# A decoder step with a streamed mixture of experts: six expert slots instead of five, the residual rows parked in memory, the conditioning weights in half blocks

## What is computed

```python
mod = silu(c) @ w_ada + b_ada                   # 1024 x 6144: shift, scale, gate, twice
h = rmsnorm(x, g1) * (1 + sc1) + sh1
z = h @ w_in                                    # 1024 x 2048: conv gates B and C, value v, S5 input u
y_conv = B * conv3(C * v)
y_ssm = glu(gelu(s5(u)))                        # 32 groups, 64 complex states, scan over positions
x = x + gt1 * (concat(rmsnorm(y_conv), rmsnorm(y_ssm)) @ w_out)
h = rmsnorm(x, g2) * (1 + sc2) + sh2
x = x + gt2 * moe(h)                            # top 1 of 4 groups, then top 2 of 8 experts in it
y = rmsnorm(x, final_g)
```

## Time and profile before

| | |
|---|---|
| time, three runs | 652.00, 662.49, 662.91 us; median 662.49 us |
| the profiled execution | 654.28 us, of which the span from first to last instruction is 652.5 us |
| TensorE: busy, mean granted clock | 519.0 us (80% of the span), 0.914 |
| DVE, ACT, POOL busy | 268.3, 111.7, 81.9 us |
| moved by DMA | 168.96 MB, mean 259 GB/s; 414 to 419 GB/s in the slices from 392 to 587 us but one (412) |
| chain that ended last | PE 49%, DMA 26%, SP's queue 11%, DVE 8% |

### The profile page before, as it was taken

The page is one execution under the profiler, slowest core; times in us unless marked ns, Lnnn a source line. Parts: engine busy times, 40 slices in busy tenths (PEclk is TensorE's granted clock), DMA queues, the critical chain, the costliest instruction groups (busy, mean ns, idle before and its releaser), DMA issues.

```text
span 652.5 us, 8666 instructions
## 1 busy us (share of the span) xinstructions
PE 519.0 (80%) x3412; PEld 311.5 (48%) x3412; DVE 268.3 (41%) x603; ACT 111.7 (17%) x205; POOL 81.9 (13%) x117
## 2 busy tenths in 40 slices
PE   0658999988999979999933999977787878768291
PEld 0546898867788856445532344333232323223040
DVE  6429928894163351574555222222121202111246
ACT  4502171110000343222212001010000001000012
POOL 4020003000011320210012021111111111100001
PEclk9977999999999979999955899999797979979786
DMA  8995037757598878010196499999999999994343
GB/s 293 331 303 224 1 131 74 256 200 303 177 248 30 224 288 341 0 41 32 38 383 258 161 396 414 414 416 417 417 416 416 419 412 416 415 416 201 119 181 137
DMA packets 33545, 168.96 MB, mean 259 GB/s; under 512 B 6572, under 2 KB 8828, under 8 KB 22160
## 3 DMA queue, kind: packets, MB, share of 16 engines
q1 hardware_dynamic: 26128, 150.69, 62.7%
q0 software_dynamic: 7376, 17.71, 8.9%
HBM read 161.89 MB, written 13.18 MB: 268 GB/s over the span
## 4 chain that ended last, share of the span: by engine, by line
PE 49%; DMA 26%; SPq 11%; DVE 8%; issue 2%; POOL 1%; ACT 1%; DVEq 0%; POOLq 0%; ACTq 0%
DMA arena<-in_w_ada 11%; PE bank L1400 11%; DMA arena<-in_w_exp 10%; PE bank L1646 10%; PE bank L1537 7%; SPq L425 6%; SPq L417 5%; PE bank L1675 4%; PE bank L1384 3%; DMA arena<-in_w_in 3%; PE bank L1528 2%; PE bank L1702 2%; DVE arena L859 1%; PE bank L1629 1%; PE bank L1578 1%
## 5 line engine op out<-in xcount | busy, mean ns | idle before, releaser
L1646 PE MATMUL bank<-arena 128*64 128x512 f32 x512 | 126.2, 649 | 31.7 <-DMA arena<-in_w_exp 30.6
L1400 PE MATMUL bank<-arena 128*128 128x272 f32 x512 | 122.3, 400 | 3.9 <-DMA arena<-in_w_in 3.9
L1400 PEld LDWEIGHTS bank<-arena 128*128 128x128 f32 x512 | 98.0, 193 | 25.9 <-DMA arena<-in_w_in 4.2
L859 DVE TENSOR_TENSOR arena<-arena 128x16 f32<-128x16 f32 (+12 forms) x196 | 93.7, 478 | 23.6 <-ACT arena L728 13.7
L1646 PEld LDWEIGHTS bank<-arena 128*64 128x64 f32 x512 | 43.3, 149 | 113.3 <-issue 99.7
L1675 PE MATMUL bank<-arena 128*64 128x512 f32 x256 | 58.5, 597 | 11.8 <-DVE arena L1283 11.8
L1275 DVE TENSOR_TENSOR arena<-arena,bank 128x256 f32<-128x256 f32 x16 | 6.7, 422 | 142.6 <-ACT arena L814 142.6
L1537 PE MATMUL bank<-arena 128*128 128x512 f32 x128 | 56.7, 596 | 0.0
L1384 PE MATMUL bank<-arena 128*32 128x128 f32 x768 | 28.2, 310 | 34.0 <-DMA arena<-in_w_ada 31.5
L591 POOL DMA_INDIRECT expert_rows<-arena x16 | 16.1, 1009 | 219.9 <-DVE arena L1291 205.1
L1384 PEld LDWEIGHTS bank<-arena 128*32 128x32 f32 x768 | 24.8, 126 | 37.9 <-issue 23.2
(11 more groups left out here) (180 smaller groups left out, 446.7 us busy)
## 6 DMA issues: line engine op xcount, KB each, us to landing
arena<-in_w_exp SPq DMA_DIRECT2D x64, 1024.0 KB, 22.9
arena<-in_w_exp SPq DMA_DIRECT2D x64, 512.0 KB, 19.4
arena<-in_w_ada SPq DMA_DIRECT2D x12, 2048.0 KB, 9.0
arena<-in_w_in SPq DMA_DIRECT2D x4, 2048.0 KB, 12.0
arena<-in_w_out SPq DMA_DIRECT2D x2, 2048.0 KB, 16.6
arena<-expert_rows SPq DMA_DIRECT2D x4, 1024.0 KB, 8.2
arena<-in_x_prompt SPq DMA_DIRECT2D x4, 512.0 KB, 7.6
arena<-in_x_prompt POOLq DMA_DIRECT2D x4, 512.0 KB, 12.4
```

What stands on the lines that cost most here:

```text
L859: link(V.tensor_tensor(out, a, b, op))
L1400: ins = mm(bk[:, 0:HTOK], w[:, k, P * f:P * (f + 1)], hT[:, k, HTOK * h:HTOK * (h + 1)], start=(k == 0), stop=(k == KT - 1))
L1646: ins = mm(out[CAP * e:CAP * (e + 1), :], x[:, 4 * h + kk, CAP * e:CAP * (e + 1)], slot[(2 * c + e) % NSLOT][h][:, kk, :], start=(h == 0 a ...
```

## The change

1. **Front loads at once.** `ada(3)` gets a buffer of its own (at 133) and the first block of `w_in` another (at 80, the later place of the matrix `T`), so that SP issues the first five blocks without a wait, and the small late loads go behind the second block of `w_in`. POOL zeroes `T` only after `zu` has read the block there; before, it did so at the start.
2. **Halves through a ring.** `ada(4)` to `ada(11)` are loaded as two halves of 1 MB each into a ring of three places of 8 KB. SP waits less often for the block just before; PE waits for a half at a time.
3. **Constants first.** POOL builds the routing constants ahead of the root of the branch norms, and DVE prepares the token numbers ahead of its wait for that root.
4. **Six slots.** Behind each `h2` store POOL also stores the tile's rows `x1` in memory (`x1_rows`). Their place becomes most of a sixth slot, loaded ahead after SP has seen all five stores. At the end of the expert stage SP loads the rows back (`x1_back`, into slot 4) after the 15th pair's `down`, and ACT and DVE use these.
5. **ACT asks for down weights.** From the seventh expert on SP issues only gate and up loads; ACT issues a coming pair's four down loads after its copy `y_half` of the pair that frees the place.

```diff
-NSLOT = 5
+NSLOT = 6
...
-STREAM = [("ada", 0, 0, None), ("ada", 1, 1, None), ("ada", 2, 2, None), ("ada", 3, 0, ("ada", 0)), ("in", 0, 1, ("ada", 1)),
+STREAM = [("ada", 0, None, "b0", None), ("ada", 1, None, "b1", None), ("ada", 2, None, "h0", None), ("ada", 3, None, "late", None),
+          ("in", 0, None, "T", None), ("ada", 4, 0, "h0", ("ada", 2)), ("ada", 4, 1, "h1", ("ada", 2)),
...
-        block_buf = [at(16 * b, KT, 512) for b in range(NBUF)]
+        block_buf = {"b0": at(0, KT, 512), "b1": at(16, KT, 512), "h0": at(32, KT, 512), "h1": at(40, FT, 512),
+                     "h2": at(137, FT, 512), "T": at(80, KT, 512), "late": at(133, KT, 512)}
...
-                slot_at(116, 133, 124, 141)]
+                slot_at(116, 133, 124, 141), slot_at(149, 157, 165, 177)]
...
+        x1_back = [at(k, D) for k in (116, 120, 124, 133, 137)]
...
                 for k in range(NSLOT, NE):
                     sp.wait_ge(gu_done, count(p, (k - NSLOT) // 2 + 1))
                     load(k)
-                    sp.wait_ge(down_done, count(p, (k - NSLOT) // 2 + 1))
-                    load_down(k)
+                sp.wait_ge(down_done, count(p, PAIRS - 1))
+                sp.dma_start(at(116, 2, D), x1_d[0:2 * P, :].rearrange("(i p) d -> p i d", i=2)).then_inc(x1_landed, 16)
+                for i, (t0, n) in enumerate(TILES):
+                    if i >= 2:
+                        sp.dma_start(x1_back[i][0:n, :], x1_d[t0:t0 + n, :]).then_inc(x1_landed, 16)
...
             load(4)
             load_down(4)
+            sp.wait_ge(x1_stored, 16 * 5)
+            load(5)
+            load_down(5)
             load_rest(0)
...
-            pool.memset(T, 0.0).then_inc(T_zero, 1)
...
+            wait_full(pool, job("zu", (FT - 1, 1)))
+            pool.memset(T, 0.0).then_inc(T_zero, 1)
...
                 pool.dma_start(h2_d[t0:t0 + n, :], h2[p % 2][0:n, :]).then_inc(h2_stored[p % 2], 16)
+                pool.dma_start(x1_d[t0:t0 + n, :], x1[0:n, i, :]).then_inc(x1_stored, 16)
...
+            def load_next_down(c):
+
+                for k in (2 * c + NSLOT, 2 * c + 1 + NSLOT):
+                    if k < NE:
+                        s = k % NSLOT
+                        for h in range(2):
+                            a = KT * 512 + D * h
+                            act.dma_start(slot[s][2 + h], t["w_exp"][k][:, a:a + D]).then_inc(down_full[s], 16)
...
                     y_half(p, c)
+                    load_next_down(c)
...
+                    if c >= 4 and k % FT == 0:
+                        w = block_at("ada", c, k // FT)
```

More of the change, by code:

```diff
@@ L302, in build @@
         par_in, conv_in, wr_in, x_again = (sem(n) for n in ("par_in", "conv_in", "wr_in", "x_again"))
-        block_in = [sem(f"block_in{b}") for b in range(NBUF)]
+        block_in = {b: sem(f"block_in_{b}") for b in BUFS}
         late_row_in = sem("late_row_in")
@@ L398, in quarters @@
                     sp.dma_start(dst[32 * j:32 * (j + 1), :, :], src[0:1, :, j, :].partition_broadcast(32)).then_inc(done, 16)
-            for kind, c, b, after in STREAM:
+            for kind, c, part, b, after in STREAM:
                 if after is not None:
                     wait_full(sp, job(*after))
-                kts = FT if kind == "glu" else KT
+                kts = FT if kind == "glu" or part is not None else KT
                 src = t["w_glu"] if kind == "glu" else t["w_" + kind][c]
+                if part is not None:
+                    src = src[:, FT * 512 * part:FT * 512 * (part + 1)]
                 sp.dma_start(block_buf[b][:, 0:kts, :], src.rearrange("p (k n) -> p k n", k=kts)).then_inc(block_in[b], 16)
@@ L408, in _ @@
                     quarters(g1_q, t["g1"], 2, row_in)
-                if kind == "ada" and c == 2:
+                if kind == "in" and c == 1:
                     quarters(late_bias, t["b_ada"][:, 4 * 512:12 * 512], 8, late_row_in)
@@ L453, in _ @@
                     sp.wait_ge(pass_open, p + 1)
-                    for k in range(NSLOT):
+                    load(0)
+                    load_down(0)
+                    sp.wait_ge(x1_landed, p * 64)
+                    for k in range(1, NSLOT):
                         load(k)
@@ L544, in _ @@
             pool.dma_start(br, t["b_router"]).then_inc(wr_in, 16)
-            pool.wait_ge(msm_ready, 1)
-            pool.tensor_tensor(rstd_m, ms_m, half, ALU.pow).then_inc(mrstd_ready, 1)
+            wait_full(pool, job("ss", 0))
             link(pool.memset(tri, 1.0))
@@ L558, in _ @@
             pool.sem_inc(moe_consts, 1)
+            pool.wait_ge(msm_ready, 1)
+            pool.tensor_tensor(rstd_m, ms_m, half, ALU.pow).then_inc(mrstd_ready, 1)
             for p, i in enumerate(ORDER):
@@ L1346, in finish @@
                 dve.wait_ge(rstd2_ready, i + 1)
-                V.scalar_tensor_tensor(out=x2[i][0:rows, :], in0=x1[0:rows, i, :], scalar=rstd[0:rows, i:i + 1],
+                V.scalar_tensor_tensor(out=x2[i][0:rows, :], in0=x1_back[i][0:rows, :], scalar=rstd[0:rows, i:i + 1],
                                        in1=fg[0:rows, :], op0=ALU.mult, op1=ALU.mult).then_inc(y_ready, 1)
@@ L1372, in _, with block_at @@
             open_job.next = 0
-            def block_at(kind, c=0):
-                b, uses = BLOCK_OF[(kind, c)]
+            def block_at(kind, c=0, part=None):
+                b, uses = BLOCK_OF[(kind, c, part)]
                 pe.wait_ge(block_in[b], 16 * uses)
```

34 lines of the change are left out of this document (21 added, 13 removed).

## The result

The changed kernel takes 633.55 us (median of four runs, 633.4 to 640.3) against 660.35 for the kernel before in the same group of runs: a ratio of 0.967 (0.962 to 0.972). The ratios, with their 95% intervals, are estimated from the fast runs of both kernels and are not the quotient of the two medians. The forecast was 641.8, range 633 to 654.

A forecast was written before the change was run, and what follows sets the result against it. TensorE was taken to bind half of the end, late loads the rest, with DMA binding the expert stage. 654.28 - 7.5 - 5.7 - 0.6 - 7.6 + 6.0 - 1.4 + 4.3 = 641.8 us, range 633 to 654.

The forecast's parts named there:

- the forecast's own case: Whole kernel: all terms come as summed, 641.8 us, counted as 638 to 647; chance 0.43.
- the first rival: Expert stage: sixth slot pays in full, gather slips through, ends keep cover; 631.5 us; in full or part, chance 0.29.
- front loads at once: Front: fourth conditioning block and w_in land earlier, first projection at 43.65 instead of 51.20 us; -7.5 us.
- ring of halves: Projections: second halves always land within a part's 7.5 us, so eight cycles take 75.7 instead of 81.4 us; -5.7.
- sixth slot, bytes: Expert stage: one expert's 3.15 MB no longer pass while the stream bounds, at 416 GB/s; -7.6 us.
- first gather slower: Before the expert stage: first gather meets the sixth slot's loads, 10.1 us instead of 4.1; +6.0 us.
- start of the stream: Expert stage's start: SP no longer holds gate and up loads behind a wait for down; -1.4 us (0 to -2.7).
- order at the end: Expert stage's end: fewer bytes left to cover PE's last two pairs; +4.3 us, between 0 and 7.4.
- so down weights run ahead: Expert stage: ACT's queue isn't served behind SP's, leaving only 4.2 MB instead of 7.3 near the end.
- Front or ring keep less: Front and projections: w_in behind POOL's tiny loads, halves slow as blocks; 651.0, one alone 645.3 or 647.5; chance 0.20.
- No sixth load ahead: Expert stage: last x1 store lands after the first gate_up, so no bytes ahead, no slower gather; 643.4 us; chance 0.03.
- ACT stalls: Expert stage: four issues block ACT above 10.2 us, delaying silu and copies; at 3.5 us each, 691 us; chance 0.05.

The follow-up runs named there:

- e4: Changed kernel with the eight small late loads back behind the third conditioning block, ahead of the fourth: 641.41 us, ratio 0.969.
- e5: Changed kernel with both halves of a conditioning block waiting until the whole block ahead of them is done: 636.28 us, ratio 0.974.
- e2: Changed kernel with five slots, no sixth expert loaded ahead: 639.64 us, ratio 0.968.
- e3: Changed kernel with the sixth slot's loads held back until PE has turned the first gathered rows: 632.18 us, ratio 0.954.
- e10: Kernel before, with only ACT asking for the down weights added: 654.03 us against 658.38, ratio 0.993.
- e1: Changed kernel with SP asking for the down weights too, in the old order: 635.38 us, ratio 0.962.
- e9: Changed kernel unaltered, run once more in another group of runs: 636.65 us against 658.38 for the kernel before, ratio 0.967.
- e7: Changed kernel with the residual rows read back after the last gate_up, not the 15th down: 635.91 us, ratio 0.972.
- e6: Changed kernel with SP asking for all weights, both experts of a pair at once, ACT for none: 635.54 us, ratio 0.972.
- e8: Changed kernel with SP asking for all in pairs, sixth slot loaded after the first gather, rows read back after the last gate_up: 629.92 us, ratio 0.963.
- e11: Changed kernel with SP asking for all in pairs and sixth slot loaded after the first gather, rows read back as before: 629.76 us, ratio 0.957.
- e12: Changed kernel with SP asking in pairs, sixth slot after the first gather, rows read back late, run again: 631.49 us, ratio 0.959.

## Why the prediction was right, and where it was wrong

The direction held; the range held at its very edge, 633.55 us with a lower end of 633. The forecast was 8.4 us too high in its own frame (641.8 against a profiled 633.4): 1.9% less was forecast, 3.3% came, and the 638 to 647 of the forecast's own case was missed. The time falls among the first rival's (631.5, or 636 to 638 with one of the two costs), and that rival had half of it right: the gather did not slip through, but the end did not lose its cover. By its terms:

| term | predicted | measured | by |
|---|---|---|---|
| front loads at once | -7.5 | -7.1 | trace; e4 takes it back |
| ring of halves | -5.7 | -6.1 | trace; e5 splits it, 3.6 and 2.5 |
| constants first | -0.6 | -0.6 | trace |
| sixth slot, bytes | -7.6 | -7.2 | e2 against e3 |
| first gather slower | +6.0 | +4.3 | trace; e3 takes 3.7 back |
| start of the stream | -1.4 | -1.4 | e10; 1.2 of it e1 gives back |
| order at the end | +4.3 | -2.8 to +1.3 | what is left of the stage |

The last line is worked out: the stage from first to last `gate_up` is 11.4 us shorter in the first profile and 7.3 in e9; the bytes and the start make 8.6 of it, so the end is between -2.8 and +1.3; in e10 it is +0.6. Two profiles of one kernel lie 4.1 us apart in this stage, so its terms are no surer than that. Of the 8.4 us the end makes 7.1 and the gather 1.7; the other terms nearly cancel.

**The step that failed** is "so down weights run ahead". I read it from the gathers' median of 10.1 us against SP's 22.9: that a second queue is not served behind the first. The gathers are small and come one at a time; a queue that is itself full of megabytes is another thing. ACT's loads land after 29.2 us, SP's after 28.3: they wait alike, and since ACT asks later, behind its copy of a result, its weights are the ones that PE waits for, from the eighth `down` to the 15th. At the end the price is not a lost cover of 7.4 us, but a wait of 1.9 to 4.6 us in front of the 15th `down` wherever ACT asks (the changed kernel twice, e2 to e5, e7, e10), with the last `gate_up` behind it. Where SP asks for all (e1, e6, e8, e11, e12) that `down` waits for no weights, and the last `gate_up` waits 0.6 to 4.8 us for its own. What the end costs then differs from one execution to the next, by the clock too. In the first profile the last `gate_up` still waited for its own weights, so the wait of 2.59 us ahead of it cost little, and PE stayed at full clock; in e9 it waited for none, and behind 4.55 us PE ran at half, 2.7 us more for `down` alone. What I said would be seen, a last `gate_up` ending 6 to 9 us after the last expert byte, was 3.65 in the first profile and 13.3 in e9 (574.85 to 588.11).

**The start** came as priced, and for the reason given: the first load's own latency stayed and the wait in order went. But no second queue was needed for it, as e6 shows.

**The first gather** was the right mechanism with the size too large: it shared the DMA engines with what was left of the loads and landed after 8.36 us, not the median of the stream.

**The front** came as worked out, though not by the path I named: `w_in` and not `hT` ended the wait, and PE did wait for the fourth block, 2.60 us. `w_in` came 3.6 us later than the 40.5 that I worked out, and `hT` half a us earlier than the 43.65: the two paths are a us apart, so the number held, in part by luck.

**The rivals.** *Front or ring keep less*: no. *No sixth load ahead*: no; without it (e2) the gather is fast again and the stage longer. *ACT stalls*: its first half is there. Four issues took up to 9.40 us, close to the 8.7 that I worked out, and silu came 1.1 us late (1.6 worked out); the point at which it decides, 10.2 us, was not reached, and e1 and e6, where ACT asks for nothing, are no faster.

The Trainium skill ("DMA: Bandwidth & Descriptors", "Issuing engines are not separate DMA queues") says that what several engines ask for runs on the same 16 DMA engines and interleaves. This the traces bear out: 417 GB/s with two queues and 416 with one, and equal times to landing. That sentence speaks against the order that I gave the two queues' bytes. It adds that only the sequencer's time to issue is saved; here it was not saved but handed to ACT, 9.40 us for four issues, and what was gained at the start came from a wait in order that fell away (353 GB/s with it in e1, 377 and, with SP alone, 380 without).

**What stays open.** The two medians of the first group differ by 26.8 us, the two profiles by 20.8, because the profiled execution of before (654.28) lies 6 us below its median. Single runs of before spread from 652 to 665 us, of the changed kernel from 633 to 640. For the changed kernel e9 shows one place where that arises; for the kernel before no run shows in which stage its longer executions lose. ACT's loads are half the size of SP's, and ACT asks for half the bytes; whether two queues land alike with other sizes no run here shows. What the order of use is worth by itself at the end (e11 has it only together with e3's edit) is open, too.

## What to carry to other kernels

In a stage that bytes bind, price three things apart: when the stream can start, how many bytes it has to move, and what work is left behind the last byte; e2 starts 3.9 us early and still ends 5.4 late, since it has one expert more to load. Here a second queue changed the order of bytes, not their rate, and was worth only the wait in order that it removed, which one queue could do as well (e6). Don't load ahead across a small transfer that everything waits for (e3). Compare how two streams begin from the event that frees them, not from the same clock time. Halving a load so that work can begin on its first half was worth more here than asking for it earlier (3.6 against 2.5 us).

## What the hardware showed that was not expected

- Two queues with different sizes of load (1 MB and 0.5 MB) come to the same time from issue to landing, 28.3 and 29.2 us with six slots, 26.1 and 25.8 with five, and the engine that asks later is the one whose weights PE waits for.
- The same wait of PE, in two executions of one kernel, was 2.59 us with the granted clock at 1.00 behind it, and 4.55 us with 0.50 behind it; the two differ by 6.1 us, mostly through that end. An earlier wait of 1.78 us had 0.68 behind it.
- The GLU product began behind three waits of about 1 us, at a granted clock of 0.52 from 227 to 233 us (0.70 from 240 to 246 before), and took 1.2 us longer than before with no change to it.
